# Unread products of a constant block on TensorE between the last output product and the first expert

## The reference

```python
x = x + g1 * m                                   # m: the mixer's output projection
h = rmsnorm(x, p['g_norm2'][i]) * (1 + sc2) + sh2
gp = jax.nn.softmax((h @ w_rg + b_rg), axis=-1)  # 4 groups; the best one is taken
el = jnp.einsum('nd,gde->nge', h, w_re) + b_re   # 8 experts a group; the best two are taken
...
hid = jax.nn.silu(xblk @ w_g[e]) * (xblk @ w_u[e])
yb = hid @ w_d[e]                                # for each block of tokens of expert e
x = x + g2 * y
```

## Time and profile before

| | us |
|---|---|
| median of 3 runs (lowest, highest) | 1968.13 (1967.0, 1976.59) |
| the profiled execution's own time | 1974.81 |
| its span, first to last instruction | 1972.8 |
| mean granted TensorE clock, share of full | 0.913 |
| TensorE matmul busy | 1565.3 (79%) |
| VectorE busy | 603.5 (31%) |
| ScalarE busy | 233.6 (12%) |

### The profile page before, as it was taken

The page is one execution under the profiler, slowest core; times in us unless marked ns, Lnnn a source line. Parts: engine busy times, 40 slices in busy tenths (PEclk is TensorE's granted clock), DMA queues, the critical chain, the costliest instruction groups (busy, mean ns, idle before and its releaser), DMA issues. The chain is left out here.

```text
span 1972.8 us, 18415 instructions
## 1 busy us (share of the span) xinstructions
PE 1565.3 (79%) x6508; PEld 714.8 (36%) x6508; DVE 603.5 (31%) x1147; ACT 233.6 (12%) x448; POOL 213.5 (11%) x337
## 2 busy tenths in 40 slices
PE   4899987769598877877778389999597888787872
PEld 1445534545443322322233144555442233232330
DVE  1469545543521111211111432023521112111114
ACT  2111133311100000000000121101100000000001
POOL 0022010000011111111111000000021111111110
PEclk9999997869689999999999799999689899998996
DMA  8744202410569999999999655320679999999994
GB/s 303 237 146 178 86 11 86 150 43 31 204 271 419 421 420 421 421 421 420 419 418 413 257 200 213 129 107 31 246 280 421 420 420 420 420 418 415 421 393 185
DMA packets 125785, 558.92 MB, mean 283 GB/s; under 512 B 22877, under 2 KB 23702, under 8 KB 72234
## 3 DMA queue, kind: packets, MB, share of 16 engines
q1 hardware_dynamic: 96176, 518.64, 65.3%
q10 hardware_dynamic: 18170, 18.58, 2.9%
q0 software_dynamic: 11392, 21.08, 2.9%
HBM read 546.63 MB, written 26.28 MB: 290 GB/s over the span
## 5 line engine op out<-in xcount | busy, mean ns | idle before, releaser
L1453 PE MATMUL psum_pair_B<-weight_ring,scratch 128*64 128x512 f32 x2176 | 537.6, 651 | 138.0 <-DMA weight_ring<-w_up 127.0
L1453 PEld LDWEIGHTS psum_pair_B<-weight_ring,scratch 128*64 128x64 f32 x2176 | 181.5, 149 | 489.4 <-issue 486.0
L1471 PE MATMUL psum_pair_C<-weight_ring,scratch 128*64 128x512 f32 x1088 | 248.4, 597 | 38.5 <-issue 36.1
L1116 DVE TENSOR_TENSOR scratch<-psum_pair_B,scratch 128x256 f32<-128x256 f32 x68 | 28.9, 424 | 652.9 <-ACT scratch L728 652.9
L570 POOL DMA_INDIRECT expert_rows<-scratch,scatter_rows x68 | 69.5, 1022 | 848.6 <-DVE scratch L1128 848.6
L1368 PE MATMUL psum_pair_A<-scratch,weight_ring 128*128 128x128 f32 (+1 forms) x512 | 141.7, 435 | 2.5 <-DVE scratch L952 2.5
L1368 PE MATMUL psum_pair_B<-scratch,weight_ring 128*128 128x128 f32 (+1 forms) x512 | 143.6, 439 | 0.0
L1471 PEld LDWEIGHTS psum_pair_C<-weight_ring,scratch 128*64 128x64 f32 x1088 | 85.8, 136 | 154.3 <-issue 154.3
L728 ACT ACTIVATE scratch<-psum_pair_B 128x256 f32<-128x256 f32 x68 | 26.0, 383 | 940.9 <-PE psum_pair_B L1453 940.9
L1179 DVE SCALAR_TENSOR_TENSOR weight_ring<-weight_ring,params 128x655 f32<-128x655 f32 x120 | 114.0, 950 | 5.0 <-DVE gates_by_token L921 0.9
L1368 PEld LDWEIGHTS psum_pair_B<-scratch,weight_ring 128*128 128x128 f32 x512 | 79.1, 192 | 70.7 <-issue 70.7
(11 more groups left out here) (273 smaller groups left out, 1284.2 us busy)
## 6 DMA issues: line engine op xcount, KB each, us to landing
weight_ring<-w_gate SPq DMA_DIRECT2D x68, 2048.0 KB, 18.2
weight_ring<-w_up SPq DMA_DIRECT2D x68, 2048.0 KB, 22.7
weight_ring<-w_down SPq DMA_DIRECT2D x68, 2048.0 KB, 22.8
weight_ring<-w_ada SPq DMA_DIRECT2D x24, 2048.0 KB, 8.9
weight_ring<-w_in_e SPq DMA_DIRECT2D x5, 2048.0 KB, 13.0
scratch<-expert_rows SPq DMA_DIRECT2D x10, 1024.0 KB, 9.1
weight_ring<-w_in_o SPq DMA_DIRECT2D x4, 2048.0 KB, 19.1
h_rows<-scratch ACTq DMA_DIRECT2D x10, 512.0 KB, 3.2
```

The costliest lines, as they stand in the source:

```text
L1453: ins = mm(PB[B_][CAP * q:CAP * (q + 1), 512 * par:512 * par + 512].rearrange("p (u n) -> p u n", u=2), XGT[par][:, at:at + CAP], w[:, :, ...
L1471: ins = mm(PB[C_][CAP * q:CAP * (q + 1), 512 * par:512 * par + 512], HIDT[par][:, at:at + CAP], wd[:, j, 512 * q:512 * (q + 1)], start=(j ...
```

## The change

At four places of each layer TensorE is given products of the first 512 columns of the constant block `SQ` (identity, ones and two more matrices) with the identity. They are written into the first half of pair C, and nothing reads them. There are 2 after the loop of the tail, 1 after the last tile's transposes, 8 after the ranks have been read by VectorE, and 2 after the table: 13 a layer, 26 matmul instructions. Before the first and the third group there is a wait until pair C has been read. Nothing else changes.

```diff
+            def keep_busy(n):
+
+                for _ in range(n):
+                    mm(PB[C_][:, 0:512], ident, SQ[:, 0:512], start=True, stop=True)
+
             def tail(l, tag, cat):
...
                         logits(t - 1)
                     if t >= 2:
                         router_product(t - 2)
+                after(pe, "out", l, NT - 1, 0)
+                keep_busy(2)
                 router_product(NT - 2)
                 logits(NT - 1)
+                keep_busy(1)
                 fill(pe, "logit", l)
                 filled(router_product(NT - 1), "logit", l)
...
                 filled(ins, "rank", l)
+                after(pe, "rank", l)
+                keep_busy(8)
                 pe.wait_ge(sig("one_hots"), l + 1)
...
                 filled(ins, "table", l)
+                keep_busy(2)
                 pe.wait_ge(sig("row_weights"), l + 1)
```

## The result

The changed kernel takes 1952.45 us (median of 7 runs, 1949.62 to 1960.17), the kernel before 1968.13 (1967.0 to 1976.59): a ratio of 0.9921, 95% interval 0.9895 to 0.9946, 15.7 us less by the medians. The profiled execution took 1951.57 us, 1949.6 of it span, at a mean granted clock of 0.927 instead of 0.913.

What follows compares the result with a forecast made beforehand. Bound: TensorE's half-clock chain between output products and first gate and up products, while DMA idles. Savings of 10.4 and 10.1 us total 20.5; less 1.3 and 2.7, 16.5 off 1968.1 gives 1951.6 us, range 1943 to 1964.

Steps and rivals of the forecast that it cites:

- nothing comes of it: Rival, chance 0.11: mostly-zero products do not raise the clock enough, or the weight stream takes the gain back; 1968 us.
- The four waits: Places of the added products in each layer: all hidden in the likely case, cost 0, up to 0.4 us a layer.
- T: Time from the start of the eight products after the ranks to the clock's rise; from 5.8 us on, work is exposed.
- slower: Rival, chance 0.05: the eight products after the ranks run at 1.2 GHz throughout; 5.4 us a layer exposed, 1979 us.
- Router products and transposes together: Layer 0, tiles 3 and 4, at the high clock: 1.36 + 0.87 + 1.89 us saved; layer 1: 1.61 + 0.89 + 1.89.
- Table: Twenty table instructions after the ranks, at the high clock: 2.15 us saved in layer 0, 1.9 in layer 1.
- Row weights to transposes: After the table, up to the block's transposes: 1.4 us saved in layer 0, 1.2 in layer 1, limited by the gather.
- gate and up products: First block's 32 instructions at the high clock, 9.69 to 7.0 us: 2.7 us saved in layer 0, 2.6 in layer 1.
- one renewed fall: Clock falling again before the gate and up products in one of the two layers: 2.7 us taken off the saving.
- one of the signs by which I had said that I would be wrong: After the change, the gate and up products still begin at clock 0.50 in both layers.
- Rival 1: Chance 0.20: clock falls in the row-weight stretch and before the last router product; only 10.1 us saved, 1958 us.
- The rule of the Trainium skill on transposes: Transposes do not count as busy for the clock gate: 2.8 us a layer lost, 15 us saved instead of 20.5.

Runs made afterwards that it cites:

- e7_last_waits: Changed kernel plus half a product more after the table, half after the row weights, three quarters after the first block's transposes: 1953.12 us, ratio 0.9911.
- the tail's products alone: Changed kernel without the 8 products after the ranks and the 2 after the table, only the 2 + 1 earlier ones kept: 1965.0 us, ratio 0.9983.
- twelve products: Changed kernel with 12 products instead of 8 after the ranks: 1958.21 us, ratio 0.9941.
- the second half alone: Changed kernel with only the 8 products after the ranks and the 2 after the table, without the earlier 2 + 1: 1960.26 us, ratio 0.9966.
- the narrow products: Changed kernel with each added product of 512 columns replaced by two of 32 columns: 1972.8 us, one run.

## Why the prediction was right

- **The time.** 1951.6 forecast, 1952.45 measured, inside the range. Partly luck: 16.5 us were to be saved, and the stretches show 13.8. The times have an interval of 10.6 to 20.7 us and can't tell the two apart; what lies between 13.8 and 15.7 is within their spread.
- **Where the gain lies.** The idle DMA stretch bounds the layer, and what was saved there was kept: the stream of weights and all behind it took 834.4 and 525.5 us, against 833.8 and 526.7 before. The stretch itself got shorter by 6.9 us a layer, not by the 10 forecast. The rival "nothing comes of it" fell in both its forms.
- **The four waits.** They hid all the added work, as worked out: 0.34, 1.02 and 0.75 us of wait are left behind the second, third and fourth group. T, the time until the clock is back under the eight products, was some 3.4 us in layer 0. The longest such group of sixteen instructions in any profile took 9.47 us (layer 1 of e7_last_waits), by the prediction's 6.9 + T/2 a T of 5.1, still under its 5.8. So "slower" had no ground. Its price of 10.8 us also left out the tail: the tail's products alone saved 3.4 us a layer at both router products, whatever the eight behind them do. That work which runs over a wait is paid, twelve products showed.
- **The size by items, layer 0.** Router products and transposes together: 4.1 forecast, 3.5 measured (14.14 to 10.59 us after the last output product). Table: 2.15 against 1.97. Both miss for the same reason, the price at 2.4 GHz: 1.71 was read where the sixteen stand between output products without a wait, and in the changed kernel, with the clock at 1.00, they took 1.98 and 1.95. Why is not shown. Row weights to transposes: 1.4 against 0.96 (7.32 to 6.36 us from the table's end). The gather is the limit as forecast, and lands 5.2 us after the table's end as forecast; but the four transposes behind it took 1.13 us instead of 0.6, at the clock that had just fallen. Layer 1: 4.4 against 3.8, 1.9 against 1.7, and 1.2 against 0.5, since the chain shows 4.11 us for the gather there.
- **The term that was mis-sized:** gate and up products, 2.7 and 2.6 forecast, 0.4 and 0.9 measured. I allowed for one renewed fall in one layer before them; in both profiles of the changed kernel it fell in both. That is 4 of the 6.7 us between 20.5 and 13.8. It is also one of the signs by which I had said that I would be wrong: the gate and up products still begin at 0.50 in both layers. The median came out close because this loss of 4.0 us happens to be as large as what I had taken off for other executions (1.3) and for one fall (2.7), and because the times are no finer. Rival 1 named this place and what stands there, narrow products and short waits in a row, and this part of its loss came, 4.0 of 5.3 us; the other part, the last router product, did not. The kernels with all waits filled had 7.09 us in both layers: with the clock kept the term has the size forecast, and the change as made did not keep it.
- **The rule of the Trainium skill on transposes.** By it 2.8 us a layer would have been lost; the transposes raised the clock, as the row said.

Open is why the work ahead of the change takes its different courses, and why the kernel with the tail's products alone shows half of its stretches' gain in time. Its profiled execution had the slowest course of all (505.4), but its other nine runs have no profile.

## What to carry to other kernels

Where a chain of short TensorE steps with waits between them is on the path, read the pace of one kind of instruction at both levels of the clock before looking at anything else: here the clock was up to nearly half of the price of six steps (3.60 us against 1.95). Unread products into a free part of PSUM in those waits can buy it back, if they end before the wait does. Here sixteen instructions of 512 columns did, and 64 of 128, while 32 of 32 columns in the same wait did not. Look for the waits that are left: the longest step lost its clock in both layers, and filling them all was worth 1.5 to 2.1 us more in each. With a change under 1%, compare the stretch in the profiles as well as the times, since two executions of one program differed by 6.9 us, half the gain, before the change even began.

## What the runs showed that I had not expected

The stretch of the kernel before repeats within 0.2 us between layers and executions (53.94 and 53.76, 53.93 and 53.93, and again 53.94 and 53.76 with the narrow products). Its parts do not: in the second execution of before the row weights took 4.30 and 4.51 us instead of 3.95 and 4.04, and the gate and up products 9.33 and 8.56 instead of 9.69 and 9.60. Nothing here shows why the sum comes out the same. Meanwhile the attention stage before it, with the same instructions, varies by 5.5 us. And with the same products before them the gate and up products took 7.09 us in one layer and 9.78 in the other of one execution (the second half alone).
